# Index scores of a sparse attention in head pairs on two halves of the rows, between forget-gate products; four more low halves made by transfers

## The reference, cut to what matters

```python
h = rmsnorm_2(x, norm_mix[layer])
hq, hf, hi, hg, sq, sk, sv, iq, ik, iw, mq = split_in(h @ w_in[layer])
# dsa_mix, one block of 128 queries, 8 index heads of 64
s = jnp.einsum('bqhd,bsd->bqhs', iqb.astype(f32), ik32)
score = jnp.einsum('bqh,bqhs->bqs', iwb, jax.nn.relu(s))
score = jnp.where(visible[None], score, -jnp.inf)
_, idx = lax.top_k(score, topk)            # topk = 128
# hgrn2_mix
log_f = jnp.logaddexp(jnp.log(lb), jnp.log1p(-lb) + jax.nn.log_sigmoid(z))   # z = hf, lb = 0
qf = jax.nn.silu(q.astype(f32))                                              # q = hq
```

## Time and profile before

| | |
|---|---|
| median of 3 runs | 1542.08 us (1541.72 to 1542.87) |
| the profiled execution's own time | 1541.8 us |
| its span in the profile | 1540.0 us |
| PE busy | 1521.7 us (99%) |
| DVE busy | 860.6 us (56%) |
| ACT busy | 641.3 us (42%) |
| POOL busy | 24.1 us (2%) |
| DMA engines, mean | 103 GB/s |

### The profile page before, as it was taken

How to read it: one execution, slowest core, us unless ns; L and a number is a source line. 1 busy time by engine, 2 the same in 40 slices (tenths; PEclk the granted TensorE clock), 3 DMA queues, 4 the chain that set the end, 5 groups by cost and what they waited for, 6 DMA issues and landing times. The chain is left out here.

```text
span 1540.0 us, 20083 instructions
## 1 busy us (share of the span) xinstructions
PE 1521.7 (99%) x7670; PEld 1268.5 (82%) x7670; DVE 860.6 (56%) x1321; ACT 641.3 (42%) x888; POOL 24.1 (2%) x32
## 2 busy tenths in 40 slices
PE   7999999999999999999999999999999999999999
PEld 7888667888888888888888868999888888888887
DVE  5443565444456877777434778878564543444222
ACT  6442444322245444444333555686653322322210
POOL 0000000000000000000000000010000000000000
PEclk9999999999999999999999999999999999999999
DMA  9313212232233133222333223254312322222232
GB/s 363 132 55 109 103 56 82 83 109 94 98 113 133 55 110 109 83 107 82 137 109 128 69 83 113 56 124 106 91 65 82 110 84 107 87 103 96 95 109 82
DMA packets 25386, 158.33 MB, mean 103 GB/s; under 512 B 2819, under 2 KB 3331, under 8 KB 8300
## 3 DMA queue, kind: packets, MB, share of 16 engines
q1 hardware_dynamic: 23228, 150.01, 27.5%
q0 software_dynamic: 2016, 7.34, 2.5%
q10 hardware_dynamic: 80, 0.13, 0.0%
HBM read 147.87 MB, written 2.13 MB: 97 GB/s over the span
## 5 line engine op out<-in xcount | busy, mean ns | idle before, releaser
L1202 DVE TENSOR_TENSOR w_lo<-raw,w_hi 128x2048 fp32r<-128x2048 f32 x109 | 249.8, 2292 | 347.3 <-ACT w_hi L644 347.2
L1952 PE MATMUL bank<-h_hi,w_hi 128*128 128x512 f32 x1096 | 431.5, 394 | 1.1 <-DVE cy L1544 0.8
L1954 PE MATMUL bank<-h_hi,w_lo 128*128 128x512 f32 x1096 | 427.0, 390 | 0.0
L1953 PE MATMUL bank<-h_lo,w_hi 128*128 128x512 f32 x1096 | 426.7, 389 | 0.0
L644 ACT ACTIVATE w_hi<-raw 128x2048 fp32r<-128x2048 f32 x123 | 235.0, 1910 | 321.7 <-PE bank L1954 307.4
L1952 PEld LDWEIGHTS bank<-h_hi,w_hi 128*128 128x128 f32 x1096 | 205.6, 188 | 45.3 <-issue 2.8
L1954 PEld LDWEIGHTS bank<-h_hi,w_lo 128*128 128x128 f32 x1096 | 205.3, 187 | 43.7
L1953 PEld LDWEIGHTS bank<-h_lo,w_hi 128*128 128x128 f32 x1096 | 205.5, 188 | 42.0 <-issue 0.2
L1952 PE MATMUL bank<-a_hi,w_hi 128*128 128x512 f32 x352 | 136.9, 389 | 0.0
L1953 PE MATMUL bank<-a_lo,w_hi 128*128 128x512 f32 x352 | 136.9, 389 | 0.0
L1954 PE MATMUL bank<-a_hi,w_lo 128*128 128x512 f32 x352 | 136.9, 389 | 0.0
(11 more groups left out here) (315 smaller groups left out, 2005.2 us busy)
## 6 DMA issues: line engine op xcount, KB each, us to landing
raw<-weights SPq DMA_DIRECT2D x128, 1024.0 KB, 4.8
w_lo<-raw POOLq DMA_DIRECT2D x14, 512.0 KB, 5.0
toep<-bias_scratch SPq DMA_DIRECT2D x8, 448.0 KB, 4.6
x<-xT SPq DMA_DIRECT2D x2, 1024.0 KB, 12.7
x_tok<-x_tok SPq DMA_DIRECT2D x1, 2048.0 KB, 13.8
mem2T<-mem2T SPq DMA_DIRECT2D x2, 1024.0 KB, 5.3
outT<-x SPq DMA_DIRECT2D x8, 256.0 KB, 4.2
lead<-lead SPq DMA_DIRECT2D x2, 512.0 KB, 4.7
```

What stands on the lines that cost most here:

```text
L1202: nc.vector.tensor_tensor(w_lo[PLACE[m]][:, :], raw[m % 2][:, :], w_hi[PLACE[m]][:, :].bitcast(F32), ALU.subtract).then_inc(lo_ready, 1)
L1952: nc.tensor.matmul(o, lh, rh, start=first, stop=False)
L1953: nc.tensor.matmul(o, lh, rl, start=False, stop=False)
L1954: return nc.tensor.matmul(o, ll, rh, start=False, stop=last)
```

## The change

It makes one tile `ik` with the key in both halves of the rows, in place of the two padded ones, and two memsets of POOL go. The scores are made in pairs of an even and an odd head, with 64 rows each, and behind each pair come two of the 24 products of the `hf` tiles 1 to 3, so that there are 12 rounds of a pair and two products. The transposes `turn_km` stand behind them and use banks 4 and 5. ACT rounds the second load of `hf` ahead of the scores, and the first load of `hq` between them. DVE does the low half of the second `hf` load, the norms of `hf`, the mask and three steps of `top_keys` between its score additions. `BY_DMA` begins at `hq`: the low halves of both `hq` loads, of `sq` and of `sk` are made by ACT and transfers, as those behind them are, and the four splits of DVE go. POOL's transfers are cut into three groups, with the memsets of `kmT_odd` and `skT_odd` between them. No arithmetic of the result changes.

```diff
@@ -93,7 +93,7 @@
-BY_DMA = range(FIRST["mq"], FIRST["w_out_2"] + 1)
+BY_DMA = range(FIRST["hq"], FIRST["w_out_2"] + 1)
@@ -236,7 +236,7 @@
-    tiles("turn_km", 2, (2, 3))
+    tiles("turn_km", 2, (4, 5))
@@ -371,7 +371,7 @@
-        ik = [at(f"ik{s}", AR + (40 + 2 * s) * K, [S]) for s in range(2)]
+        ik = at("ik", AR + 40 * K, [S])
@@ -578,6 +578,18 @@
+            def add_lows(first, last):
+                for n_ in range(first, last):
+                    m = BY_DMA[n_]
+                    if n_:
+                        pool.wait_ge(lo_added, 32 * n_)
+                    for part in range(2):
+                        cut = slice(part * SLOT // 2, (part + 1) * SLOT // 2)
+                        pool.wait_ge(minus_hi, 2 * n_ + part + 1)
+                        nc.gpsimd.dma_start(w_lo[PLACE[m]][:, cut], raw[m % 2][:, cut], accum_op=ALU.add
+                                            ).then_inc(lo_added, 16)
@@ -603,20 +611,15 @@
             pool.wait_ge(padded, 1)
             nc.gpsimd.memset(skT[0][64:P, :, :], 0.0).then_inc(padded, 1)
             pool.wait_ge(padded, 2)
+            add_lows(0, 1)
             pool.wait_ge(*completion(("turn_km", 1)))
             nc.gpsimd.memset(kmT[1][0:64, :, :], 0.0).then_inc(padded, 1)
             pool.wait_ge(padded, 3)
+            add_lows(1, 2)
             pool.wait_ge(log_used, 1)
             nc.gpsimd.memset(skT[1][0:64, :, :], 0.0).then_inc(padded, 1)
             pool.wait_ge(padded, 4)
...
+            add_lows(2, len(BY_DMA))
@@ -998,8 +1001,9 @@
             wait_own(("ik", 0))
-            nc.scalar.dma_start(ik[1][64:P, :], ik[0][0:64, :]).then_inc(ik_odd_in, 16)
+            nc.scalar.dma_start(ik[64:P, :], ik[0:64, :]).then_inc(ik_odd_in, 16)
             head_root(MT * SAH)
+            round_w(FIRST["hf"] + 1)
             ready(("iw", 0))
             act.wait_ge(rms_col, 4)
             for t in range(TT):
@@ -1012,6 +1016,10 @@
                     act.wait_ge(relu_used, w - 1)
                 keys = P * (i + 1)
                 frees(("idx", w), nc.scalar.activation(relu[w % 2][:, 0:keys], B(("idx", w))[:, 0:keys], ACT.Relu))
+                if w == 13:
+                    round_w(FIRST["hq"])
+                if w in (14, 15):
+                    minus_part(FIRST["hq"], w - 14)
@@ -1026,7 +1034,6 @@
-            round_w(FIRST["hf"] + 1)
@@ -1036,7 +1043,10 @@
             for m in range(2):
-                round_w(FIRST["hf"] + m + 2)
+                if m:
+                    round_w(FIRST["hq"] + 1)
+                    for part in range(2):
+                        minus_part(FIRST["hq"] + 1, part)
                 for t in (2 * m, 2 * m + 1):
                     wait_own(("hf", t))
                     nc.scalar.activation(abs_z[:, t * S:(t + 1) * S], lf[:, t * S:(t + 1) * S], ACT.Abs
@@ -1047,6 +1057,8 @@
             nc.scalar.activation(abs_z[:, :], abs_z[:, :], ACT.Ln, bias=1.0).then_inc(log_ready, 1)
             for m in range(2):
                 round_w(FIRST["hq"] + m + 2)
+                for part in range(2):
+                    minus_part(FIRST["hq"] + m + 2, part)
                 for t in (2 * m, 2 * m + 1):
                     wait_own(("hq", t))
                     nc.scalar.activation(qf[:, t * S:(t + 1) * S], qf[:, t * S:(t + 1) * S], ACT.Silu
@@ -1700,6 +1712,38 @@
...
+            def hide_later(i):
+                cut = sel[:, i, P * i:P * (i + 1)]
+                link(nc.vector.tensor_tensor(cut, cut, causal[:, :], ALU.add))
+            def between_scores(pair_):
+                if pair_ in (1, 2):
+                    split_part(FIRST["hf"] + 1, pair_ - 1)
+                if pair_ in (3, 5, 9):
+                    t = {3: 0, 5: 1, 9: 2}[pair_]
+                    ready(("hf", t))
+                    normal("hf", t, lf[:, t * S:(t + 1) * S])
+                if pair_ == 4:
+                    dve.wait_ge(relu_used, IDXH + 2)
+                    hide_later(1)
+                if pair_ in (6, 10, 11):
+                    r = {6: 0, 10: 1, 11: 2}[pair_]
+                    top_keys(r, r + 1)
@@ -1708,32 +1752,14 @@
+                if w % 2:
+                    between_scores(w // 2)
+            for i in (2, 3):
+                hide_later(i)
+            ready(("hf", 3))
+            normal("hf", 3, lf[:, 3 * S:4 * S])
+            top_keys(3, 10)
-...
-            for m in range(2):
-                if m == 0:
-                    split_w(FIRST["hf"] + 1)
-                for t in (2 * m, 2 * m + 1):
-                    ready(("hf", t))
-                    normal("hf", t, lf[:, t * S:(t + 1) * S])
-                split_w(FIRST["hf"] + m + 2)
-                top_keys(5 * m, 5 * m + 5)
@@ -1745,7 +1771,6 @@
-                split_w(FIRST["hq"] + m + 2)
@@ -2420,18 +2445,26 @@
             wait_all("iq", range(4))
             wait_all("ik", range(1))
             pe.wait_ge(ik_odd_in, 16)
-            pe.wait_ge(ik_padded, 2)
-            for w_, (i, h) in enumerate(IDX):
-                claim(("idx", w_))
-                done(("idx", w_), nc.tensor.matmul(B(("idx", w_))[:, 0:P * (i + 1)], iq[:, h // 2, i * P:(i + 1) * P],
-                                                   ik[h % 2][:, 0:P * (i + 1)], start=True, stop=True))
+            for w_ in range(0, len(IDX), 2):
+                for e in range(2):
+                    claim(("idx", w_ + e))
+                for e in range(2):
+                    i, h = IDX[w_ + e]
+                    rows_ = slice(64 * e, 64 * e + 64)
+                    done(("idx", w_ + e), nc.tensor.matmul(
+                        B(("idx", w_ + e))[:, 0:P * (i + 1)], iq[rows_, h // 2, i * P:(i + 1) * P],
+                        ik[rows_, 0:P * (i + 1)], start=True, stop=True))
+                for p_ in (KT + w_, KT + w_ + 1):
+                    t, kt = divmod(p_, KT)
+                    ld, key, cs = FIRST["hf"] + t // 2, ("hf", t), slice(t % 2 * P, (t % 2 + 1) * P)
+                    if kt == 0:
+                        weights(ld)
+                        claim(key)
+                    ins = product(B(key)[:, :], w(ld, 1)[:, kt, cs], w(ld, 0)[:, kt, cs], h_hi[:, kt, :], h_lo[:, kt, :],
+                                  kt == 0, kt == KT - 1)
+                    if kt == KT - 1:
+                        done(key, ins)
             turn_heads("turn_km", km_tok, M)
-            for t in range(1, 4):
-                ld = FIRST["hf"] + t // 2
-                weights(ld)
-                claim(("hf", t))
-                done(("hf", t), feature_tile(B(("hf", t)), ld, t % 2, *H))
             feature_loads("hq", 2)
```

More of the change, by code:

```diff
@@ L611, in _ @@
             pool.wait_ge(padded, 4)
-            for n_, m in enumerate(BY_DMA):
-                if n_:
-                    pool.wait_ge(lo_added, 32 * n_)
-                for part in range(2):
-                    cut = slice(part * SLOT // 2, (part + 1) * SLOT // 2)
-                    pool.wait_ge(minus_hi, 2 * n_ + part + 1)
-                    nc.gpsimd.dma_start(w_lo[PLACE[m]][:, cut], raw[m % 2][:, cut], accum_op=ALU.add
-                                        ).then_inc(lo_added, 16)
+            add_lows(2, len(BY_DMA))
         @block.scalar
@@ L1702, in _ @@
             wait_free(("iw", 0))
-            for w, (i, h) in enumerate(IDX):
-                keys = P * (i + 1)
-                wait_free(("idx", w))
-                if w:
-                    dve.wait_ge(relu_used, w)
-                nc.vector.scalar_tensor_tensor(out=sel[:, i, 0:keys], in0=relu[w % 2][:, 0:keys],
-                                               scalar=iw[:, i, h:h + 1], in1=sel[:, i, 0:keys], op0=ALU.mult,
-                                               op1=ALU.add).then_inc(relu_used, 1)
-            dve.wait_ge(relu_used, len(IDX))
-            for i in range(1, TT):
-                link(nc.vector.tensor_tensor(sel[:, i, P * i:P * (i + 1)], sel[:, i, P * i:P * (i + 1)], causal[:, :],
-                                             ALU.add))
             def top_keys(first, last):
@@ L1727, in top_keys @@
                         link(nc.vector.tensor_scalar(scores, scores, TAKEN, NEG, ALU.not_equal, ALU.mult))
[L1729 to L1732 removed]
+            def hide_later(i):
[6 more added lines that the diff above has]
+                    t = {3: 0, 5: 1, 9: 2}[pair_]
                     ready(("hf", t))
                     normal("hf", t, lf[:, t * S:(t + 1) * S])
[L1735 to L1736 removed]
+                if pair_ == 4:
[4 more added lines that the diff above has]
+                    top_keys(r, r + 1)
+            for w, (i, h) in enumerate(IDX):
+                keys = P * (i + 1)
+                wait_free(("idx", w))
+                if w:
+                    dve.wait_ge(relu_used, w)
+                nc.vector.scalar_tensor_tensor(out=sel[:, i, 0:keys], in0=relu[w % 2][:, 0:keys],
+                                               scalar=iw[:, i, h:h + 1], in1=sel[:, i, 0:keys], op0=ALU.mult,
```

(6 more changed lines are left out.)

8 lines of the change are left out of this document (2 added, 6 removed).

## The result

| | before | changed |
|---|---|---|
| median | 1541.72 us (1541.1 to 1542.87, 13 runs) | 1545.69 us (1544.89 to 1546.8, 13 runs) |
| profiled span | 1540.0 us | 1543.8 us |
| ratio, 95% interval | | 1.0025 (1.0017 to 1.0032) |

The account below looks back on a forecast made before the run. PE, busy 99% of the span, was taken to bound the kernel. Terms of -3.5, +3.0, +3.2 and -0.5 summed to +2.2 us, giving a forecast median of 1544.3 us, with an 8-in-10 range of 1539.5 to 1548.0.

Parts of the forecast that it names:

- the place of `hq`: Sign of being right: PE's first row of hq starts near 927.7; later than 929 would be wrong.
- the two waits for a DMA: Sign of being right: PE waits about 3 us for a DMA into w_lo near 939 and again near 953.
- the place of POOL's transfers: Sign of being right: POOL's first transfer of sq stands directly behind the memset of skT_odd.
- PE's own work, -3.5: From first score to first hq product, pairs dealt between products take PE 29.4 us against 32.9: -3.5 us.
- `hq` first, zero: First hq load's low half lands by 926 or 927, PE wants it at 927.7: no wait.
- `hq` second, a wait of 3.0: Second hq load's rounding stands behind ACT's memory keys; low half at 941.5, PE ready at 938.6: 3.0 us wait.
- `sq`, a wait of 3.2: POOL's sq transfers stand behind the memset awaiting the logarithm; low half at 955.6, PE at 952.4: 3.2 us wait.
- The clock's rival: PE's clock halves behind the waits of some 3 us, each costing 2.4 us more: 1546.7 to 1549.1; chance 0.13.
- The wait that goes, -0.5: At the fourth sq tile PE arrives later than ACT's tok, so its wait for tok disappears: -0.5 us.
- The chain behind is later: Rival: sk's transfers or ACT's lateness add a 1 to 2 us wait at level 0 or sk: 1545.5 to 1547; chance 0.20.
- DVE relieved, worth nothing: DVE loses four splits, 9.2 us, costed at nothing because the chain in the levels shifts with PE.
- The transfers are in time, so 1538.6: Rival: low halves land sooner, waits shrink to about 0.5 us in all, PE's gain remains: 1538.6; chance 0.12.

Follow-up runs that it names:

- Full_dealt: dve_tok with scores of 128 rows on two padded keys, dealt between the products in the same places: 1547.75 us.
- pairs_block: The kernel before with the scores in pairs of 64 rows, still in one block: 1541.91 us, ratio 1.0002.
- pool_order: The changed kernel with POOL's transfers of sq ahead of the memset of skT_odd that waits for the logarithm: 1547.34 us.
- dve_lows: The changed kernel with the four low halves (both hq loads, sq, sk) made by DVE as before: 1542.4 us, ratio 1.0 to before.
- dve_tok: dve_lows with ACT reading the first sq tile (tok) ahead of its second pair of Silu: 1545.97 us.
- log_later: both_tok with ACT's rounding and negations of sq between Exp and Ln, and DVE's first two hq norms ahead of the logarithm: 1546.15 us.
- keys_early: log_later with six of DVE's top_keys steps ahead of the logarithm instead of behind it: 1539.48 us, ratio 0.9982 to before.
- both_tok: The changed kernel with second hq load prepared ahead of memory keys, sq's transfers ahead of skT_odd's memset, tok read ahead of the second Silu pair: 1542.12 us.
- lows_only: The kernel before with the four low halves by transfers alone, the scores still in their block: 1546.47 us, ratio 1.0028.

## Why the prediction was right, and where not

The time lies in the range and 1.4 us above the point. Of the outcomes, no change had 0.48 and slower by over 0.2% had 0.39, and the ratio of 1.0025 (1.0017 to 1.0032) does not decide between these two. Of the signs that the prediction named, the place of `hq`, the two waits for a DMA and the place of POOL's transfers came as it said. Three went the other way: the clock fell behind a wait, which stands among its signs of being wrong, the wait for tok stayed, and PE's busy time fell by 1.0 us and not by 2 to 3.

- **PE's own work, -3.5.** Measured -3.13. The pair prices held: from 906.71 to the second matmul behind the pair (908.22) is 1.51, less 0.455 makes 1.05, forecast 1.06; the other two came out at 0.84 and 1.26. What was missing is the first pair, which costs 0.36 more, since it waits 0.33 for ACT's iw. Full_dealt and pairs_block confirm that the gain is the pairing's, and only when dealt.
- **`hq` first, zero.** Right: landed at 924.8, wanted at 927.6.
- **`hq` second, a wait of 3.0.** Right in mechanism and near in size: the rounding began at 930.42 instead of 930.8, and PE lost 2.6.
- **`sq`, a wait of 3.2.** The landing was right (955.06 against 955.6), and so was the cause, which pool_order shows: with the transfers ahead of the memset the wait is gone. The size was not. PE came to `sq` at 953.8 instead of 952.4, so it waited 1.3. It had lost the rest already to the clock. The two terms together cost 2.6 + 1.7 + 1.3 = 5.6, with the forecast of 6.2 for both waits at full clock.
- **The clock's rival** (0.13) did happen at the first wait, in the profiled execution, and in ten of the thirteen by their mean clock. Its premise was right, its price was not: it put 2.4 us per fall on top of the waits. Here the fall took 1.7, and the next wait was shorter by most of that, since the low half of `sq` has a date of its own. Thus 1545.7 and not 1546.7. The three executions without a fall, 1544.9 to 1545.3, come nearer to the forecast of 1544.3, which had no fall in it.
- **The wait that goes, -0.5.** This step failed, and it makes most of the miss. The prediction let ACT's tok follow the rounding of `sk` at 952.7, by 10.3. The distance held (954.09 to 964.49 is 10.4), but the rounding has to wait for the last product of `hq`, and that came late with PE: the last one starts 12.4 behind the wait instead of 10.7, because of the clock. The wait is 1.2 in place of 0.5, so +0.7 where -0.5 was put. An estimate from these rows: without the fall the rounding would begin at 952.4 and tok at 962.8, and PE could go on at 963.3, ahead of its own turn at 963.83, so that this wait would be gone as forecast. No profile of such an execution was taken.
- **The chain behind is later** (0.20). In part: +0.8 behind level 4, at the two places named above.
- **DVE relieved, worth nothing.** Right for the change as it stands: dve_lows, with the splits back on DVE, is the faster one. The chain ACT, DVE, ACT from the logarithm to z takes up PE's lead in dve_tok and log_later alike. What paid was the order of DVE's work, in keys_early; whether less work on DVE helped there too was not run.
- **The transfers are in time, so 1538.6** (0.12). This would have given the gain only if nothing else were near. Dve_lows had no late low half and took 1542.4, so the rival's sum was wrong as well: it let the whole lead of PE through the levels.

The span grew by 3.8 us where +2.2 was forecast. The 1.6 between them are 0.4 of pairs, 1.2 of tok, 0.8 behind level 4 and 0.2 of restarts, less 0.6 at the two waits and 0.5 of the earlier start. Errors of both signs stand against each other here, so part of the nearness is luck.

## What to carry to other kernels

An edit that makes the bounding engine faster in one stage moves its lead (the time by which it is early) to the next thing with a date of its own. Here that was, in this order, a low half, another low half, a read of a bank, and the first input of the levels, and taking away one wait at a time gained nothing. So list all chains that end within the lead before you value the gain, and fill idle time of the other engines from what stands behind it in their queues; and keep work with a slow tail (a negation, a transfer, its landing) off an order in which it queues behind a wait for something else.

## What the runs showed of the hardware

**A wait of 2 to 3 us can halve PE's clock, and it need not.** Behind a wait of 2.29 us dve_lows ran at 0.57 for the next 4 us, and behind one of 2.71 us both_tok kept its clock of 1.00 in the profiled execution. In pool_order one wait of 2.43 left the clock at 1.00, and one of 1.96 dropped it to 0.59. The same kernel on the same chip does one and the other: in five of eleven executions of dve_lows the mean clock was 1.0 and the time 2 us less. Nor does it take one long wait: in pairs_block the clock was 0.50 from 903.9 to 907.2, with no wait over 0.72 us in the block. Before, with no wait over 1.1 us behind the start, none of the 79 executions of that kernel measured beside these runs showed a mean clock under 1.0. The Trainium skill (TensorE: Matmul & The Clock Gate, section HAM oscillation — how this bites in real kernels) describes products that start cold again behind each wait for a DMA. The trace agrees where PE waited for `w_lo` at 941.20 [2.45], and pool_order at the same place does not.

**The same fall has different prices.** In the traces of the changed kernel and of lows_only the half clock lasted a little over 3 us among products of 512 or 256 and took 1.7 us there. Between executions of one kernel the difference was 0.6 us in the changed kernel, where the next wait took up most of it, 1.6 in lows_only and 2 in dve_lows. In front of the levels' 64-wide matmuls the half clock lasted longer: the granted clock was 0.50 from 967.7 to 977.8 in dve_tok and from 970.3 to 977.0 in log_later, with PE busy throughout. Dve_tok took 1545.97 where its one execution at full clock took 1541.05, so nearly 5 us. That the narrow matmuls are the reason is not shown.

**Two halves of the rows side by side.** With products on both sides a pair of float32 scores costs 0.84, 1.05 and 1.26 us for 256, 384 and 512 keys, 3.0 us less for all twelve than scores of 128 rows in the same places.
